# Five slots for the experts' weights instead of three, two of them in memory that the routing stage has used, one packed table of weights, and an earlier turning of the plan

## The chip, the cores and the metric

One core of one Trainium2 chip runs the whole program. The metric is the device time of one execution in microseconds (us). The kernel before took 3438.68 us (median of 3 runs, 3435.18 to 3443.06). One further execution was recorded by the profiler: it took 3445.58 us, its span (first to last instruction) is 3442.7 us. All durations below are from that execution.

## The reference, cut to what matters

Two transformer blocks stand behind each other; the second has two layers. The change touches the mixture of experts at the end of each of these two layers. It works on 512 tokens of 1024 numbers, all float32:

```python
def moe_ffn(h, router_w, router_bias, w_gate, w_up, w_down, ws_gate, ws_up, ws_down):
    scores = sigmoid(xt @ router_w)                       # 512 tokens x 64 experts
    ...                                                   # groups, then the best 8 experts of each token
    wts = wts / sum(wts) * ROUTED_SCALE
    ...
    def run_block(args):                                  # a block of tokens of one expert e
        hb = silu(xb @ w_gate[e]) * (xb @ w_up[e])        # 1024 -> 256, twice
        return (hb @ w_down[e]) * ws[:, None]             # 256 -> 1024
    ...
    shared = (silu(xt @ ws_gate) * (xt @ ws_up)) @ ws_down
    return routed + shared
```

Which experts get how many tokens is known only on the chip. An expert's weights are 3 matrices of 1024 x 256 floats, 1 MB each, 3 MB in all; there are 64 experts.

## The kernel before, in words

Each layer's mixture of experts runs in three stages: `route_tokens`, `routed_experts`, `combine`.

**`route_tokens`** normalises the tokens, scores them, picks the experts and works out a *plan*: rows of `plan` say which expert each pass serves. DVE makes the plan by some 60 small operations on columns (L2589 and near it), ends with `wide` (L2664) and counts `cols_ready`. PE turns `wide` into rows (L2477), DVE copies them into `plan` (L2671) and counts `plan_ready`. SP reads three experts' numbers from it and issues the first loads (`first_loads`, L1899 to L1905). DVE goes on to match seats with tokens (`passes.select`, L1947), PE finds the tokens of the first passes (`passes.find`, L1955 and L1958), and POOL gathers their rows. Beside this PE computes the shared expert in four products of 8 matmuls (`shared_product(j, m)`, L2443): (0,0), (1,0), then the turning of the plan, (0,1) with the first find ahead of its k = 5, the second find, (1,1). The stage's own big buffers are `hT_e`, `shared_up` and `rows_hat`, 16 KB per partition each. The next stage starts when every engine has ended this one.

**`routed_experts`** goes through rounds r = 0, 1, ... Each round has two passes of 128 seats: pass b = 0 serves one expert ("whole"), pass b = 1 serves two of 64 seats each ("first", "second"). There are 47 passes in the first of the two layers and 45 in the second; the last round has pass b = 0 alone. A pass on PE is: turn the gathered rows (L2828), `up` (gate and up matrices, L2842), turn the hidden rows (L2853), `down` (L2866). PE's order, written out by hand: up(r,0), down(r-1,1), turn, up(r,1), down(r,0), turn. Between them stand the finds of later passes. ACT and DVE empty the accumulators, and POOL gathers rows for later passes and scatters the results (L1977, L2784).

The weights lie in `experts`, `[P, 3, EXPERT]`: one slot of 24 KB per partition for each of the three parts, 16 KB of it for gate and up, 8 KB for down. SP loads them in a fixed order: `load_up(r,0)`, `load_down(r-1,1)`, `load_up(r,1)`, `load_down(r,0)`. Each call waits until PE has done the pass of the round before on that slot (L2730: `up_made`, `down_made`), then issues 1 MB DMAs, two for an `up`, one for a `down` (L1910, L1914). A 1 MB DMA writes 8 KB to each of 128 partitions, from one contiguous megabyte of HBM.

**`combine`** sums the 8 results of each token with the shared expert's product and normalises.

Of the kernel before, what the change touches and what calls it, by code (L numbers as in the profile page):

```python
# [20 lines left out]
P = 128  # L21
T = 512
TT = T // P
D = 1024
# [1853 lines left out]
class Experts:  # L1878
# [5 lines left out]
    def __init__(self, prog, ctx, l):  # L1884
        d = prog.dram
        self.l = l
        self.mem = prog.sb(ctx, "experts", [P, 3, EXPERT])
        self.holder, sems = prog.semaphores([f"{part}_loaded_{i}" for part in ("up", "down") for i in range(3)])
        self.up_loaded, self.down_loaded = sems[0:3], sems[3:6]
        self.shared = [d["ws_gate_2"][l], d["ws_up_2"][l], d["ws_down_2"][l]]  # L1890
        self.routed = [d["w_gate_2"], d["w_up_2"], d["w_down_2"]]

    def up(self, slot):
        return self.mem[:, slot, 0:4 * DK * P].rearrange("p (h k n) -> p h k n", h=2, k=DK)

    def down(self, slot):
        return self.mem[:, slot, 4 * DK * P:6 * DK * P].rearrange("p (k n) -> p k n", k=2)

    def first_loads(self, sp, plan):  # L1899


        es = [sp.value_load(plan[0:1, at:at + 1], min_val=0, max_val=EXPERTS - 1) for at in (0, P, P + 1)]
        for slot in range(3):
            self.load_up(sp, slot, es[slot])
        self.load_down(sp, self.WHOLE, es[0])  # L1905
# [7 lines left out]
    def load_down(self, sp, slot, e):  # L1913
        sp.dma_start(self.mem[:, slot, 4 * DK * P:6 * DK * P],  # L1914
                     self.routed[2][self.l, e].rearrange("(p k) n -> p (k n)", p=P)).then_inc(self.down_loaded[slot], 16)

    def retire(self, prog):
        prog.retire(self.holder, self.up_loaded + self.down_loaded)
# [393 lines left out]
def route_tokens(prog, experts, passes, late_norms, mod, xT, rw, rb, shared_down, shared_down_loaded,  # L2312
# [7 lines left out]
    nc, d = prog.nc, prog.dram  # L2320
    gain, shift = late_norms[:, 0, :], late_norms[:, 1, :]
    with ExitStack() as ctx:
        hT = prog.sb(ctx, "hT_e", [P, DK, T])
        shared_up = prog.sb(ctx, "shared_up", [P, 2, DK, FF])
        rows_hat = prog.sb(ctx, "rows_hat", [P, TT, D])
        h_tok = rows_hat
        by_turns = h_tok[:, :, :].rearrange("p t (k a) -> p t a k", k=DK)
        stats = prog.sb(ctx, "stats", [P, TT, 2, 6])
# [33 lines left out]
        with prog.stage("shared_loaded", "folded", "rows_turned", "stats_ready", "moments_ready", "root_ready", "rstd_ready",  # L2362
# [34 lines left out]
            def _(pe):  # L2397
# [38 lines left out]
                def shared_product(j, m, hook=False):  # L2436
                    for k in range(DK):
                        if hook and k == 5:
                            pe.wait_ge(s["plan_ready"], 1)
                            e = experts_of(pe, 0)[0]  # L2440
                            pe.wait_ge(s["matched"], 1)
                            passes.find(pe, 0, e, info, find_ps[0]).then_inc(s["found"], 1)
# [40 lines left out]

            @block.scalar
# [207 lines left out]
def routed_experts(prog, experts, passes, seat, info, plan, base):  # L2692
# [4 lines left out]
    with ExitStack() as ctx:  # L2697
# [12 lines left out]
        y_ps = prog.ps(ctx, "y_ps", [P, 2, T])  # L2710
        with prog.stage("matched", "found", "noted", "read_noted", "turned", "copied_dve", "copied_act",
                        "up_made_0", "up_made_1", "up_made_2", "silu_ready", "hid_ready", "hid_turned", "hid_copied",
                        "down_made_0", "down_made_1", "down_made_2", "write_noted", "y_dve", "y_act", "go", "shared_out", drains=False) as (block, s):
# [3 lines left out]
            whole, first, second = experts.WHOLE, experts.FIRST, experts.SECOND  # L2717

            def end_of(eng):

# [2 lines left out]
            def past(j, n):  # L2723

                return not isinstance(j, int) or j >= n
# [6 lines left out]
            def experts_of(eng, r, b):  # L2732

                return [eng.value_load(plan[0:1, bass.ds(at, 1)], min_val=0, max_val=EXPERTS - 1)
                        for at in ((r,) if b == 0 else (P + 2 * r, P + 2 * r + 1))]

            @block.sync
            def _(sp):
                def load_up(r, b):
                    es = experts_of(sp, r, b)  # L2740
                    if past(r, 1):
                        all_waited(sp, up_made[b], r)
                    for i, e in enumerate(es):
                        experts.load_up(sp, b + i, e)

                def load_down(r, b):
                    es = experts_of(sp, r, b)
                    if past(r, 1):
                        all_waited(sp, down_made[b], 2 * r)
                    for i, e in enumerate(es):  # L2750
                        experts.load_down(sp, b + i, e)

                end = end_of(sp)
                load_up(1, 0)
                load_down(0, 1)
                load_up(1, 1)
                load_down(1, 0)
# [6 lines left out]
                load_up(last, 0)  # L2764
                load_down(end, 1)
                load_down(last, 0)

            @block.gpsimd
            def _(pool):
# [42 lines left out]
            def _(pe):  # L2812
# [19 lines left out]
                def up(r, b):  # L2832
                    j = 2 * r + b
                    for i in range(b + 1):
                        pe.wait_ge(experts.up_loaded[b + i], 32 * (r + 1))
                    pe.wait_ge(s["copied_dve"], j + 1)
                    pe.wait_ge(s["copied_act"], j + 1)
                    if past(j, 2):
                        pe.wait_ge(s["hid_ready"], j - 1)
                    for k in range(DK):  # L2840
                        for i, part in enumerate((ALL,) if b == 0 else halves):
                            made = pe.matmul(up_ps[part, b, :].rearrange("p (h n) -> p h n", h=2), xT[:, b, k, part],  # L2842
                                             experts.up(b + i)[:, :, k, :], start=(k == 0), stop=(k == DK - 1))
                            if k == DK - 1:
                                made.then_inc(up_made[b][i], 1)

# [9 lines left out]
                def down(r, b):  # L2856
                    j = 2 * r + b
                    for i in range(b + 1):
                        pe.wait_ge(experts.down_loaded[b + i], 16 * (r + 1))
                    pe.wait_ge(s["hid_copied"], j + 1)  # L2860
                    for side in range(2):
                        if past(j, 1):
                            pe.wait_ge(s["y_dve"] if side == 0 else s["y_act"], j)
                        for k in range(2):
                            for i, part in enumerate((ALL,) if b == 0 else halves):
                                made = pe.matmul(y_ps[part, side, :], hidT[:, b, k * P + part.start:k * P + part.stop],  # L2866
                                                 experts.down(b + i)[:, k, side * 512:(side + 1) * 512],
                                                 start=(k == 0), stop=(k == 1))
                                if k == 1:
                                    made.then_inc(down_made[b][i], 1)  # L2870
# [492 lines left out]
```

## Time and profile before

| | |
|---|---|
| median of 3 runs | 3438.68 us (3435.18 to 3443.06) |
| the profiled execution | 3445.58 us, span 3442.7 us |
| PE (matmul) busy | 3097.1 us, 90% of the span |
| DVE, ACT, POOL busy | 46%, 29%, 7% |
| DMA | 739.11 MB, mean 215 GB/s over the span |
| expert loads | 137 each of gate, up and down, 1024 KB each |

The page cuts the span into 40 slices of 86 us. Slices 19 to 26 and 32 to 39 are the two `routed_experts` stages: there the DMA engines' busy share is 9 tenths in nearly each, at 350 to 410 GB/s, and PE's is 9 too. Outside them the DMA share is mostly 0 to 6 tenths. "DMA share" is the mean over the core's 16 DMA engines; above 1 it means that transfers overlapped. PEclk is the clock granted to PE as a part of its full speed; it is either full (1.0) or half.

### The profile page before, as it was taken

Reading aid. Unit: us, or ns where it says so; the run is one execution under the profiler, and the core shown is the slowest. Engines: PE = TensorE matmul, PEld = TensorE weight load, DVE = VectorE, ACT = ScalarE, POOL = GpSimd, SP = SyncE. Lnnn points to the kernel's source line nnn. Section 1 sums busy time; section 2 is a strip of 40 time slices with the busy share of each in tenths; the row PEclk is TensorE's granted clock in tenths of the full one; section 3 lists DMA queues with packets and bytes.
Section 4 is the critical chain, followed back from the end, with each engine's and each line's share of the span. In section 5 each row is a group of like instructions: output and inputs, shape, how many; then the busy total and the mean of one; then the engine's idle time right before and its main releaser. Section 6 shows DMA issues by size and latency. Waiting matters only on the chain. (4 is left out here: it accounts for less than half of the span.)

```text
span 3442.7 us, 44956 instructions
## 1 busy us (share of the span) xinstructions
PE 3097.1 (90%) x14116; PEld 1988.1 (58%) x14117; DVE 1596.6 (46%) x4079; ACT 983.0 (29%) x2055; POOL 252.1 (7%) x237
## 2 busy tenths in 40 slices
PE   7888989989999889989999899969899799999995
PEld 4555668878777667864444444366587444444444
DVE  2575466657566365444223323264734532323236
ACT  4565352333233244331111111133632211111111
POOL 0000000011000000000111111100000011111112
PEclk9899999999999999988999999989999899999997
DMA  5201126644543412316999999771031399999985
GB/s 207 75 2 50 48 70 189 209 159 151 184 148 129 131 28 56 104 37 249 402 406 409 399 394 406 305 292 44 26 94 57 149 394 412 396 391 403 386 353 241
DMA packets 283481, 739.11 MB, mean 215 GB/s; under 512 B 25197, under 2 KB 164655, under 8 KB 228555
## 3 DMA queue, kind: packets, MB, share of 16 engines
q1 hardware_dynamic: 231211, 619.79, 47.4%
q0 software_dynamic: 26784, 67.15, 4.9%
q10 hardware_dynamic: 25344, 50.33, 4.3%
q8 instruction: 82, 1.34, 0.2%
q14 instruction: 60, 0.49, 0.0%
HBM read 709.92 MB, written 57.67 MB: 223 GB/s over the span
## 5 line engine op out<-in xcount | busy, mean ns | idle before, releaser
L2842 PE MATMUL up_ps<-experts,x_turned 128*64 128x512 f32 (+1 forms) x2192 | 684.2, 624 | 99.4 <-DMA experts<-in_w_up_dram 80.2
L318 DVE TENSOR_TENSOR pieces_lo<-weights,pieces_hi 128x512 fp32r<-128x512 f32 (+1 forms) x468 | 319.0, 686 | 461.9 <-ACT pieces_hi L312 461.2
L2842 PEld LDWEIGHTS up_ps<-experts,x_turned 128*64 128x64 f32 (+1 forms) x2192 | 264.8, 161 | 449.0 <-issue 444.4
L312 ACT CAST pieces_hi<-weights 128x512 fp32r<-128x512 f32 (+1 forms) x468 | 284.4, 615 | 584.8 <-PE gate_ps L330 174.0
L2866 PE MATMUL y_ps<-experts,hid_turned 128*64 128x512 f32 (+1 forms) x1096 | 338.3, 601 | 2.0 <-issue 2.0
L2997 DVE TENSOR_TENSOR hid_seats<-up_ps,gated 128x256 f32<-128x256 f32 x92 | 56.2, 611 | 566.0 <-ACT gated L2919 566.0
L328 PE MATMUL gate_ps<-h_hi,pieces_hi 128*128 128x512 f32 x624 | 248.7, 399 | 19.3 <-DVE pieces_lo L318 19.3
L2919 ACT ACTIVATE gated<-up_ps 128x256 f32<-128x256 f32 x92 | 35.3, 384 | 761.4 <-PE up_ps L2842 761.4
L329 PE MATMUL gate_ps<-h_lo,pieces_hi 128*128 128x512 f32 x624 | 245.9, 394 | 0.0
L330 PE MATMUL gate_ps<-h_hi,pieces_lo 128*128 128x512 f32 x624 | 245.7, 394 | 0.0
L2866 PEld LDWEIGHTS y_ps<-experts,hid_turned 128*64 128x64 f32 (+1 forms) x1096 | 115.2, 155 | 217.6 <-issue 217.6
L328 PE MATMUL products<-h_hi,pieces_hi 128*128 128x512 f32 x464 | 196.7, 424 | 30.6 <-DVE pieces_lo L318 30.6
L330 PE MATMUL products<-h_hi,pieces_lo 128*128 128x512 f32 x464 | 187.2, 404 | 0.0
L329 PE MATMUL products<-h_lo,pieces_hi 128*128 128x512 f32 x464 | 186.6, 402 | 0.0
L2784 POOL DMA_INDIRECT results<-y_seats,write_at x92 | 92.8, 1009 | 873.6 <-ACT y_seats L2934 873.6
L1947 DVE TENSOR_SCALAR seats<-lists,base,seat 128x64 fp32r<-128x64 f32 (+1 forms) x588 | 146.5, 325 | 20.6 <-issue 20.3
L2934 ACT ACTIVATE y_seats<-y_ps,share 128x512 f32<-128x512 f32 x92 | 63.4, 689 | 310.4 <-PE y_ps L2866 310.4
L328 PEld LDWEIGHTS gate_ps<-h_hi,pieces_hi 128*128 128x128 f32 x624 | 119.1, 191 | 45.0 <-DVE pieces_lo L318 20.5
L845 ACT ACTIVATE prob<-prob,low 128x512 f32<-128x512 f32 (+5 forms) x224 | 123.9, 553 | 66.8 <-DVE low L876 65.9
L2988 DVE COPY x_turned<-turn_ps 128x512 f32<-128x512 f32 x92 | 63.6, 692 | 164.2 <-PE turn_ps L2828 164.2
L328 PEld LDWEIGHTS products<-h_hi,pieces_hi 128*128 128x128 f32 x464 | 90.1, 194 | 82.8 <-issue 40.0
L330 PEld LDWEIGHTS gate_ps<-h_hi,pieces_lo 128*128 128x128 f32 x624 | 119.0, 191 | 25.6
(454 smaller groups left out, 4930.8 us busy)
## 6 DMA issues: line engine op xcount, KB each, us to landing
experts<-in_w_gate_dram SPq DMA_DIRECT2D x137, 1024.0 KB, 8.9
experts<-in_w_up_dram SPq DMA_DIRECT2D x137, 1024.0 KB, 15.6
experts<-in_w_down_dram SPq DMA_DIRECT2D x137, 1024.0 KB, 16.6
ada_weights<-in_w_ada_dram ACTq DMA_DIRECT2D x48, 1024.0 KB, 5.3
rows_sb<-results SPq DMA_DIRECT2D x16, 2048.0 KB, 26.3
weights<-in_w_in_dram SPq DMA_DIRECT2D x57, 512.0 KB, 4.2
weights<-in_w_in_dram SPq DMA_DIRECT2D x12, 2048.0 KB, 12.2
weights<-in_w_out_dram SPq DMA_DIRECT2D x6, 2048.0 KB, 8.8
```

The source lines that it names most:

```text
L312: act.copy(self.like(view, self.hi[:, i % self.BUFFERS, :, :]), view).then_inc(s["hi_ready"], 1)
L318: dve.tensor_tensor(lo, view, hi.bitcast(F32), ALU.subtract).then_inc(s["lo_ready"], 1)
L328: pe.matmul(bank, self.hi[:, b, k, :], x_hi[:, k0 + k, :], start=(start and k == 0), stop=False)
L329: pe.matmul(bank, self.hi[:, b, k, :], x_lo[:, k0 + k, :], start=False, stop=False)
L330: last = pe.matmul(bank, self.lo[:, b, k, :], x_hi[:, k0 + k, :], start=False, stop=(stop and k == n - 1))
L845: act.activation(prob[:, u % 6, 0:x["n"]], prob[:, u % 6, 0:x["n"]], ACT.Exp, bias=low[:, u % 8:u % 8 + 1], scale=-1.0, accum_out=mass[:, ...
L1947: last = dve.tensor_scalar(self.seats[:, b, t, part], prog.count[:, 0:part.stop - part.start], firsts[i], seat[:, t, bass.ds(e, 1)], ALU.a ...
L2784: pool.indirect_dma_start(d["results"], bass.IndirectOffsetOnAxis(ap=write_at[:, b:b + 1], axis=0), y[:, b, :], None, bounds_check=last_ro ...
L2842: made = pe.matmul(up_ps[part, b, :].rearrange("p (h n) -> p h n", h=2), xT[:, b, k, part], experts.up(b + i)[:, :, k, :], start=(k == 0), ...
L2866: made = pe.matmul(y_ps[part, side, :], hidT[:, b, k * P + part.start:k * P + part.stop], experts.down(b + i)[:, k, side * 512:(side + 1) ...
L2934: act.activation(y[:, b, 512:1024], y_ps[:, 1, :], ACT.Copy, scale=share[:, bass.ds(j, 1)]).then_inc(s["y_act"], 1)
L2988: dve.tensor_copy(xT[:, b, 0:4, :].rearrange("p k n -> p (k n)"), turn_ps[:, 0, :]).then_inc(s["copied_dve"], 1)
```

## The change

The host packs, for each layer and expert, the three matrices behind each other by partition (`experts_by_partition`, 24 KB per partition), so that gate and up are one 2 MB DMA with 16 KB per partition. `experts` has five slots. "Whole" and "first" have two each, chosen by the round's parity (`place`), "second" has one. Slots 3 and 4 are also the memory of `hT_e`, `shared_up` and `rows_hat` (`spare`). SP's order of loads is new, with waits on PE of an older round for the doubled parts, a wait for the landing of the part's load before, and a count `asked` ahead of each load. PE reads a doubled part at an address that depends on the round's register. In `route_tokens` PE turns the plan after k = 1 of product (1,0), finds the first pass's tokens after k = 1 of product (0,1) and the second's after its k = 4.

```diff
+def experts_by_partition(given):
+    parts = [given[name].reshape(LAYERS, EXPERTS, P, -1) for name in ("w_gate_2", "w_up_2", "w_down_2")]
+    return np.concatenate(parts, axis=3)
...
-        self.mem = prog.sb(ctx, "experts", [P, 3, EXPERT])
+        self.mem = prog.sb(ctx, "experts", [P, 5, EXPERT])
...
+    def place(self, part, r):
+        return 2 if part == self.SECOND else 3 * (r & 1) + part
+    def spare(self):
+        return self.mem[:, 3:5, :].rearrange("p i n -> p (i n)")
+    def up(self, part, r):
+        slot = self.place(part, r)
+        return self.mem[:, bass.ds(slot, 1), 0:4 * DK * P].rearrange("p s (h k n) -> p (s h) k n", h=2, k=DK)
...
-    def load_up(self, sp, slot, e):
-        for m in range(2):
-            at = 2 * m * DK * P
-            sp.dma_start(self.mem[:, slot, at:at + 2 * DK * P],
-                         self.routed[m][self.l, e].rearrange("(p k) n -> p (k n)", p=P)).then_inc(self.up_loaded[slot], 16)
+    def load_up(self, sp, part, r, e):
+        sp.dma_start(self.mem[:, bass.ds(self.place(part, r), 1), 0:4 * DK * P].rearrange("p s n -> p (s n)"),
+                     self.routed[e, :, 0:4 * DK * P]).then_inc(self.up_loaded[part], 16)
...
-        hT = prog.sb(ctx, "hT_e", [P, DK, T])
-        shared_up = prog.sb(ctx, "shared_up", [P, 2, DK, FF])
-        rows_hat = prog.sb(ctx, "rows_hat", [P, TT, D])
+        spare = experts.spare()
+        hT = spare[:, 0:DK * T].rearrange("p (k n) -> p k n", k=DK)
...
+                        if (j, m, k) == (1, 0, 2):
+                            turn_plan()
+                        if (j, m, k) == (0, 1, 2):
+                            find_first()
+                        if (j, m, k) == (0, 1, 5):
+                            find_second()
...
                 shared_product(0, 0)
                 shared_product(1, 0)
-                pe.wait_ge(s["cols_ready"], 1)
-                pe.wait_ge(s["h_copied"], 2 * TT)
-                for i in range(4):
-                    last = pe.matmul(plan_ps[:, i, :], wide[:, i, :], prog.ident[:, :], start=True, stop=True)
-                last.then_inc(s["plan_turned"], 1)
-                shared_product(0, 1, hook=True)
-                pe.wait_ge(s["matched"], 2)
-                passes.find(pe, 1, None, info, find_ps[1]).then_inc(s["found"], 1)
+                shared_product(0, 1)
                 shared_product(1, 1)
...
-                with sp.Fori(2, last) as r:
-                    load_up(r, 0)
-                    load_down(r - 1, 1)
-                    load_up(r, 1)
-                    load_down(r, 0)
...
+                def load_up(part, r, freed, e):
+                    if past(freed, 1):
+                        sp.wait_ge(up_of[part], freed)
+                        sp.sem_inc(s["asked"], 1)
+                    if part != second:
+                        sp.wait_ge(experts.up_loaded[part], 16 * r)
+                    sp.sem_inc(s["asked"], 1)
+                    experts.load_up(sp, part, r, e)
...
+                def both(r):
+                    n = r + 1
+                    pair = two(n)
+                    load_up(second, n, n, pair[1])
+                    load_down(whole, n, r, one(n))
+                    load_up(whole, n + 1, n, one(n + 1))
+                    load_up(first, n + 1, n, two(n + 1)[0])
+                    load_down(first, n, r, pair[0])
+                    load_down(second, n, n, pair[1])
+
+                load_up(whole, 1, 0, one(1))
+                pair = two(0)
+                load_down(first, 0, 0, pair[0])
+                load_down(second, 0, 0, pair[1])
+                load_up(first, 1, 0, two(1)[0])
+                both(0)
+                with sp.Fori(1, end - 1) as r:
+                    both(r)
...
-                        pe.wait_ge(experts.up_loaded[b + i], 32 * (r + 1))
+                        pe.wait_ge(experts.up_loaded[b + i], 16 * (r + 1))
...
-                                             experts.up(b + i)[:, :, k, :], start=(k == 0), stop=(k == DK - 1))
+                                             experts.up(b + i, r)[:, :, k, :], start=(k == 0), stop=(k == DK - 1))
```

## Rows read from the trace of the kernel before

**Rows 1.** Stretches of both layers: us, busy time (instructions), PEclk, DMA share, GB/s.
```profile
1577.00:1596.00 19.00, 14.42 (x40) 6.94 (x38) 7.83 (x29) 0.60 (x1) 2.21 (x2) 0.88 1.01 405
1596.00:1607.00 11.00, 10.17 (x25) 4.75 (x24) 3.26 (x16) 0.97 (x2) 0.00 (x0) 0.74 0.10 39
1607.00:2223.00 616.00, 568.05 (x2272) 260.83 (x2271) 188.05 (x686) 87.85 (x182) 92.05 (x91) 0.98 0.98 398
2223.00:2236.00 13.00, 11.08 (x35) 3.89 (x33) 2.41 (x7) 2.02 (x4) 0.99 (x1) 1.00 0.06 21
2747.00:2758.00 11.00, 9.84 (x28) 4.94 (x28) 3.84 (x16) 0.67 (x2) 0.00 (x0) 0.84 0.13 54
2758.00:3350.00 592.00, 542.83 (x2168) 246.85 (x2167) 179.43 (x655) 83.99 (x174) 87.83 (x87) 0.97 0.98 398
```

**Rows 2.** Waits, 1595 to 3360: who waited for whom, us in total, times, longest.
```profile
PE up_ps L2842 <- DMA experts<-in_w_up_dram: 80.2, 37, 3.3
...
SPq L2730 <- PE up_ps L2842: 370.7, 43, 12.2
```

**Rows 3.** Timeline of PE: start, us, instruction group, idle before it and releaser.
```profile
1608.72 7.09 PE L2842 MATMUL up_ps<-experts,x_turned 128*64 128x512 f32 x32 [0.32 <-DVE x_turned L2988]
1621.18 7.10 PE L2842 MATMUL up_ps<-experts,x_turned 128*128 128x512 f32 x16 [0.31 <-DVE x_turned L2988]
...
2219.32 7.13 PE L2842 MATMUL up_ps<-experts,x_turned 128*128 128x512 f32 x16 [0.64 <-DVE x_turned L2988]
...
2231.39 3.67 PE L2866 MATMUL y_ps<-experts,hid_turned 128*128 128x512 f32 x8 [0.98 <-issue]
...
3358.49 3.67 PE L2866 MATMUL y_ps<-experts,hid_turned 128*128 128x512 f32 x8 [0.98 <-issue]
```

**Rows 4.** DMA packets and bytes in 1577 to 2223 and in 2728 to 3350.
```profile
DMA packets 43612, 253.34 MB, mean 392 GB/s; under 512 B 8666, under 2 KB 8666, under 8 KB 16725
...
DMA packets 41728, 243.57 MB, mean 392 GB/s; under 512 B 8010, under 2 KB 8010, under 8 KB 15994
```

**Rows 5.** Stretches of 27 us with the DMA share near 1.
```profile
1821.00:1848.00 27.00, 26.17 (x110) 11.88 (x108) 9.34 (x34) 3.87 (x8) 4.05 (x4) 1.00 1.02 422
...
1928.00:1955.00 27.00, 24.62 (x104) 11.44 (x102) 8.36 (x31) 3.87 (x8) 4.05 (x4) 1.00 0.99 401
...
2250.00:2277.00 27.00, 19.36 (x141) 18.45 (x140) 23.64 (x33) 4.18 (x11) 0.00 (x0) 0.87 1.00 427
```

**Rows 6.** Timeline around the plan in the first of the two layers.
```profile
1564.74 0.43 DVE L2664 COPY wide<-chosen_unit 128x512 f32<-128x512 f32 x1
...
1565.57 0.60 ACT L2508 ACTIVATE silu<-banks 128x512 f32<-128x512 f32 x1 [13.47 <-PE banks L2443]
1572.24 1.05 PE L2477 MATMUL banks<-square,wide 128*128 128x128 f32 x8
...
1575.98 0.38 SPq L1910 DMA_DIRECT2D experts<-in_w_gate_dram  x1
...
1580.04 0.65 PE L1955 MATMUL banks<-info,seats 128*128 x4 [2.45 <-DVEq L2681]
...
1585.27 7.11 PE L2443 MATMUL banks<-hT_e,shared_up 128*128 128x512 f32 x16
```

**Rows 7.** The same in the second layer.
```profile
2717.96 0.43 DVE L2664 COPY wide<-chosen_unit 128x512 f32<-128x512 f32 x1
...
2723.69 1.05 PE L2477 MATMUL banks<-square,wide 128*128 128x128 f32 x8
```

**Rows 8.** Register work of PE's sequencer for the first find: ns min/median/max.
```profile
L1955 PEldq FUSED_REGOPS  x188: 46/46/51, 1579.9 to 3319.0; - x188
```

**Rows 9.** Gathers of POOL: times, us from issue to landing.
```profile
x_seats<-tokens,read_at POOLq DMA_INDIRECT x94, 9.1
```

**Rows 10.** Timeline: POOL gathers for pass b = 0; PE turns these rows.
```profile
2005.10 1.02 POOL L1977 DMA_INDIRECT x_seats<-tokens,read_at  x1 [2.85 <-DVE read_at L1966]
...
2026.01 1.04 PE L2828 MATMUL turn_ps<-square,x_seats 128*128 128x128 f32 x8
```

More of the change, by code:

```diff
@@ L1890, in __init__ @@
         self.shared = [d["ws_gate_2"][l], d["ws_up_2"][l], d["ws_down_2"][l]]
[L1891 to L1897, printed above, removed]
+        self.routed = d["experts_by_partition"][l]
+    def place(self, part, r):
+        return 2 if part == self.SECOND else 3 * (r & 1) + part
@@ L1899, in first_loads, with down @@
+    def spare(self):
[3 more added lines that the diff above has]
+        return self.mem[:, bass.ds(slot, 1), 0:4 * DK * P].rearrange("p s (h k n) -> p (s h) k n", h=2, k=DK)
+    def down(self, part, r):
+        slot = self.place(part, r)
+        return self.mem[:, bass.ds(slot, 1), 4 * DK * P:6 * DK * P].rearrange("p s (k n) -> p (s k) n", k=2)
     def first_loads(self, sp, plan):
         es = [sp.value_load(plan[0:1, at:at + 1], min_val=0, max_val=EXPERTS - 1) for at in (0, P, P + 1)]
-        for slot in range(3):
-            self.load_up(sp, slot, es[slot])
@@ L1905, in first_loads @@
-        self.load_down(sp, self.WHOLE, es[0])
-    def load_up(self, sp, slot, e):
-        for m in range(2):
-            at = 2 * m * DK * P
-            sp.dma_start(self.mem[:, slot, at:at + 2 * DK * P],
-                         self.routed[m][self.l, e].rearrange("(p k) n -> p (k n)", p=P)).then_inc(self.up_loaded[slot], 16)
-    def load_down(self, sp, slot, e):
-        sp.dma_start(self.mem[:, slot, 4 * DK * P:6 * DK * P],
-                     self.routed[2][self.l, e].rearrange("(p k) n -> p (k n)", p=P)).then_inc(self.down_loaded[slot], 16)
+        for part in range(3):
+            self.load_up(sp, part, 0, es[part])
@@ L2434, in turn_h, with turn_plan, find_first, find_second @@
                     last.then_inc(s["h_turned"], 1)
-                def shared_product(j, m, hook=False):
-                    for k in range(DK):
[L2438 to L2442, printed above, removed]
+                def turn_plan():
+                    pe.wait_ge(s["cols_ready"], 1)
+                    pe.wait_ge(s["h_copied"], 2 * TT)
+                    for i in range(4):
+                        last = pe.matmul(plan_ps[:, i, :], wide[:, i, :], prog.ident[:, :], start=True, stop=True)
+                    last.then_inc(s["plan_turned"], 1)
+                def find_first():
+                    pe.wait_ge(s["plan_ready"], 1)
+                    e = experts_of(pe, 0)[0]
+                    pe.wait_ge(s["matched"], 1)
+                    passes.find(pe, 0, e, info, find_ps[0]).then_inc(s["found"], 1)
+                def find_second():
+                    pe.wait_ge(s["matched"], 2)
+                    passes.find(pe, 1, None, info, find_ps[1]).then_inc(s["found"], 1)
+                def shared_product(j, m):
+                    for k in range(DK):
+                        if (j, m, k) == (1, 0, 2):
[4 more added lines that the diff above has]
+                            find_second()
                         last = pe.matmul(shared_ps[j][m], shared_up[:, j, k, m * P:(m + 1) * P], hT[:, k, :],
@@ L2712, in routed_experts @@
                         "up_made_0", "up_made_1", "up_made_2", "silu_ready", "hid_ready", "hid_turned", "hid_copied",
[L2713 removed]
+                        "down_made_0", "down_made_1", "down_made_2", "write_noted", "y_dve", "y_act", "go", "asked", "shared_out", drains=False) as (block, s):
             scattered = passes.scattered
@@ L2753, in _, with load_down @@
+                def load_down(part, r, freed, e):
+                    if past(freed, 1):
+                        sp.wait_ge(down_of[part], 2 * freed)
+                        sp.sem_inc(s["asked"], 1)
+                    if part != second and past(r, 1):
+                        sp.wait_ge(experts.down_loaded[part], 16 * r)
+                    sp.sem_inc(s["asked"], 1)
+                    experts.load_down(sp, part, r, e)
                 end = end_of(sp)
-                load_up(1, 0)
-                load_down(0, 1)
@@ L2756, in _, with one, two @@
-                load_up(1, 1)
-                load_down(1, 0)
                 last = end + 1
-                with sp.Fori(2, last) as r:
-                    load_up(r, 0)
-                    load_down(r - 1, 1)
-                    load_up(r, 1)
-                    load_down(r, 0)
-                load_up(last, 0)
-                load_down(end, 1)
-                load_down(last, 0)
+                def one(r):
+                    return experts_of(sp, r, 0)[0]
+                def two(r):
+                    return experts_of(sp, r, 1)
@@ new lines, in _ @@
+                load_down(first, 0, 0, pair[0])
[4 more added lines that the diff above has]
+                    both(r)
+                pair = two(end)
+                load_up(second, end, end, pair[1])
+                load_down(whole, end, end, one(end))
+                load_up(whole, last, end, one(last))
+                load_down(first, end, end, pair[0])
+                load_down(second, end, end, pair[1])
@@ L2768, in _ @@
+                load_down(whole, last, end, one(last))
             @block.gpsimd
@@ L2866, in down @@
                                 made = pe.matmul(y_ps[part, side, :], hidT[:, b, k * P + part.start:k * P + part.stop],
-                                                 experts.down(b + i)[:, k, side * 512:(side + 1) * 512],
+                                                 experts.down(b + i, r)[:, k, side * 512:(side + 1) * 512],
                                                  start=(k == 0), stop=(k == 1))
@@ L3356 @@
     given["x_turned"] = features_by_partition(given["x"][0])
+    given["experts_by_partition"] = experts_by_partition(given)
+    for name in ("w_gate_2", "w_up_2", "w_down_2"):
+        del given[name]
     for name, a in given.items():
```

19 lines of the change are left out of this document (7 added, 12 removed).

## The prediction, written before the result was known

> **What bounds the kernel now.** I read the page's slices first, then the stretches of the two expert stages [rows 1], the waits [rows 2] and PE's timeline [rows 3]. The page alone says "PE 90%", which would make a change of loads worthless. The stretches say more: from 1607 to 2223 and from 2758 to 3350 the DMA share is 0.98 at 398 GB/s while PE is busy 92% of the time; both are nearly full. The waits tell which is the tighter: PE waits for an expert's up weights 37 times, 80.2 us in total [rows 2]. Where it doesn't wait, one pass follows the other after 12.46 us (1608.72 to 1621.18), so a round takes 24.9 us [rows 3]. From 1608.72 to the last up at 2219.32 there are 45 passes in 610.60 us, 13.57 each, so 27.1 us a round. SP in turn waits 370.7 us for PE to free a slot [rows 2]: with one slot per part the load of a round can't start before PE has ended the same part of the round before. Thus DMA and PE hold each other up, and the DMA stands nearly idle for 11 us at each stage's start (shares 0.10 and 0.13), because the next load needs the first pass of the stage to end [rows 1].
>
> **The change, part by part.** Sums are against the profiled execution (3445.58 us, span 3442.7), which lies 6.9 us above the median of 3438.68; I take the same difference off the median.
>
> *a. More slots.* In the new order PE's end of up(n-1,1) releases loads of second up, whole down, whole up, first up, first down: 8 MB of the round's 9, and the ninth 1 MB load waits for down(n-1,1), some 17 us on, well before 8 MB are through (8 x 1.049 MB at 412 GB/s is 20 us). When PE waits for data, SP's next release is already past, so the queue doesn't run dry. I therefore price the stage as the bytes over the rate of a full queue. The bytes stay: 253.34 and 243.57 MB, gathers and scatters included [rows 4]. The rate in full stretches of 27 us lies between 401 and 422 GB/s [rows 5]; I take the middle, 412, as either end is a single stretch. 253.34/0.412 = 615 us, 243.57/0.412 = 591 us. Gaps that stay: from the end of the first loads to the new stage's first load, and once before PE's first release of "second"; I estimate 5 us together in place of the 11 and more. So 620 in place of 646 us, and 596 in place of 622: 26 us less in each layer.
>
> *b. Two 1 MB loads become one of 2 MB with 16 KB per partition.* In a full queue the bytes count, not the number of loads. The one stretch that moves 16 KB rows, `combine`'s reading of results, runs at 427 GB/s [rows 5]; that is one end. The other end is below 401: the new source steps 24 KB from row to row instead of being contiguous, which no row shows. I take 0, nearest to the rows of these loads themselves. The Trainium skill, "DMA: Bandwidth & Descriptors", section "Bandwidth", gives some 2.0 us fixed per DMA and 341 GB/s for single 1 MB transfers. By it, 137 DMAs fewer would save 274 us. By the rows, 392 GB/s with 1 MB loads over whole stages [rows 4], the fixed part is hidden behind other transfers, and the saving is 0. The trace disagrees with the rule as a sum.
>
> *c. The end of a stage.* Now PE ends 12.1 us after the last load landed (2235.06 against 2223; 3362.16 against 3350) [rows 1, 3], because PE was behind in its own order. With DMA as the bound only the last two downs (3.67 each, the first of them can start 2.5 us before the last landing) stand behind it: 6 us. That is 6 less in each layer.
>
> *d. The plan's turning.* `wide` is complete at 1565.17; product (0,0) is read from 1565.57, so it ended just before; two matmuls of the next product at 7.11/8 = 0.89 us bring PE to 1567.1 instead of 1572.24 [rows 6]: 5.1 us. In the second layer `wide` ends at 2718.39, so 2718.6 instead of 2723.69 [rows 7]: 5.1 us, here the DVE chain sets it. SP's first load follows with it (1575.98 to about 1570.9). PE's wait of 2.45 us before the first find is covered by six matmuls more (5.3 us), and the stage ends some 3 us earlier. The DMA bound counts the 5.1. The gathers are issued about 5 us earlier too, so they don't hold the stage's start.
>
> *e. Register addresses on PE.* Every matmul of a doubled part gets an address worked out from r. The find has such an operand, one register operation of 46 ns per matmul [rows 8]; an up or down matmul takes 0.44 to 0.89 us, so behind the first of a group they are hidden, at 0.1 us for each of the 4 groups of a round, 18 us in both layers. If each took several operations they could reach 0.4 us a group, 72 us. While DMA is the bound, both hide behind it (PE has 24.9 us of work in a round of about 26.5). I take 0 and keep 18 for PE's bound.
>
> *f. `asked`, waits for landing, reads of the plan on SP.* Per load they are a few operations on a queue that waits hundreds of us. The wait for the same part's load of the round before looks back at least 9 MB of loads. 0; below, a rival.
>
> *g. Gathers beside longer rows.* A gather's 4 KB rows share the DMA engines with 16 KB instead of 8 KB rows. The trace has 9.1 us to landing [rows 9]; a doubling to 18 us is the upper end. Its rows are turned 20.9 us after the issue (2005.10 to 2026.01) [rows 10], so 0.
>
> Sum: 26 + 6 + 5 = 37 us in each layer, 74 in both: 3445.6 - 74 = 3372 profiled, **3365 us** by the median.
>
> **Rivals.**
>
> *A. PE becomes the bound.* If the full queue gives 427 GB/s as in `combine`'s stretch, DMA needs 593 and 570 us, 42 us less again, and PE can't follow. PE's own floor: 45 passes at 12.46 us are 561 instead of 610.6, so 50 less, and 3 at the start, 53; for the second layer the same. 106 less, plus 18 of register work: 88 less, **3351 us**. For it: the single stretches at 422. Against: the mean of both stages, 398 at a share of 0.98.
>
> *B. The new source layout is slower (other side).* Place: each 16 KB and 8 KB row read from HBM at a pitch of 24 KB. The gain of 74 is used up when 497 MB take 74 us more than 1206, at 388 GB/s, 6% under 412. At 380 GB/s it is 102 more: 28 slower, **3467 us**. For it: nothing shows this pattern. Against: rows of 8 KB and more are long already. The Trainium skill, same page, section "Latency and other measured facts", reports such a loss for row pitches of 2 MiB and more at powers of two. By that rule a 24 KB pitch costs nothing. No run here shows it.
>
> *C. The full queue has only the 401 GB/s end.* Then 632 and 607 us, 33 more: 41 less, **3398 us**. For it: 401 stands in a stretch with a share of 0.99. Against: the share above 1 where it is 422.
>
> *D. SP blocks its own queue:* one of its waits for a landing holds all loads behind it, and only the earlier start is left, some 10 us: **3429 us**. Against: part f.
>
> **Chances.** Forecast 0.56, A 0.19, C 0.13, D 0.04, B 0.08. What this kernel's measurement can tell from no change is 0.2%, 7 us. D is half faster, half the same. So faster 0.90, same 0.02, slower 0.08. Range: from PE's floor without register work and a little beyond (106 less is 3333, I take 3336) to C, 3400; outside are B, D and the tails.
>
> **What would show it.** Right: the DMA share is 1.0 from the stage's start, with no 11 us hole at 1596; each stage's bytes at about 412 GB/s; PE's waits for loads are less than 80 us and stand before `down` of pass b = 1 rather than before its up; `wide` to the plan's turning under 2.5 us; half-clock stretches rarer. For A: waits of PE for DMA near 0 and 12.5 to 12.9 us a pass. For B: share 1 and under 390 GB/s. For D: a low share while SP waits for a landing. Wrong altogether would be a PE that waits neither for data nor for DVE and still needs more than 13.2 us a pass: then the register addresses cost what e puts at its upper end.

## The result: 1% faster, two fifths of what was forecast

The changed kernel takes **3405.93 us** (median of 4, 3400.05 to 3411.81) against 3437.66 for the kernel before (4 runs, 3435.18 to 3443.06): ratio **0.991** [0.990, 0.992], 32 us less. Forecast were 74 less, 3365, in a range of 3336 to 3400. The direction was right, the size wrong, and the time lies outside the range. The profiled execution took 3406.53 us, its span 3404.4.

Stretches of the kernel after, in the columns of [rows 1]: from the first weight load until first passes begin, the 11 us that follow, the rest until the last load has landed, and what is left; first layer, then second.

```profile
1568.00:1590.00 22.00, 18.45 (x54) 8.78 (x53) 9.86 (x37) 1.18 (x2) 2.21 (x2) 0.94 0.98 400
1590.00:1601.00 11.00, 10.65 (x35) 5.46 (x35) 2.63 (x10) 1.24 (x3) 0.97 (x1) 0.80 1.01 427
1601.00:2201.00 600.00, 554.96 (x2260) 249.11 (x2261) 186.46 (x683) 86.92 (x180) 91.08 (x91) 1.00 0.97 400
2201.00:2213.00 12.00, 10.66 (x34) 3.69 (x32) 2.40 (x7) 1.38 (x4) 0.99 (x1) 1.00 0.06 22
2702.00:2722.00 20.00, 16.45 (x51) 7.96 (x49) 7.78 (x28) 1.18 (x2) 2.08 (x2) 0.97 0.97 404
2722.00:2733.00 11.00, 11.00 (x28) 5.31 (x28) 2.79 (x13) 0.38 (x1) 0.00 (x0) 0.75 1.01 425
2733.00:3311.00 578.00, 530.22 (x2161) 238.01 (x2160) 177.89 (x649) 83.92 (x174) 87.84 (x87) 1.00 0.97 398
3311.00:3327.00 16.00, 13.40 (x40) 4.98 (x38) 3.84 (x13) 2.02 (x4) 0.99 (x1) 1.00 0.12 43
```

The hole where [rows 1] have it is filled: shares 1.01 and 1.01 for 0.10 and 0.13. A shorter one has taken its place, some 14 us later when counted from the first load, inside the long stretches. These lines show it, then what lies behind it, then (last line) the same middle in the kernel before:

```profile
1603.00:1609.00 6.00, 6.00 (x27) 2.25 (x24) 0.42 (x1) 0.38 (x1) 0.90 (x1) 1.00 0.35 118
1620.00:2190.00 570.00, 526.16 (x2160) 235.78 (x2160) 176.49 (x643) 83.06 (x172) 87.05 (x86) 1.00 0.99 407
...
1620.00:2213.00 593.00, 546.02 (x2185) 250.27 (x2185) 179.53 (x656) 84.14 (x175) 89.06 (x88) 0.98 0.99 402
```

In the second layer the short hole lies at 2737 to 2743 (share 0.45). Behind the holes the rate is 407 GB/s at a share of 0.99 where it was 402 at 0.99: more slots, with the longer rows, have made the middle hardly faster. A stage's loads take 632 and 610 us (646 and 621 before) where the forecast had 620 and 596.

Waits from 1585 to 3330, in the columns of [rows 2]:

```profile
PE y_ps L2917 <- DMA experts<-xperts_by_partition_dram: 38.4, 28, 2.3
PE up_ps L2893 <- DVE x_turned L3039: 32.2, 61, 1.5
PE up_ps L2893 <- DMA experts<-xperts_by_partition_dram: 23.8, 31, 0.8
...
SPq L2778 <- PE y_ps L2917: 344.5, 45, 14.0
```

TensorE still waits 62.2 us for loads (38.4 + 23.8), only 18 less than the 80.2 of [rows 2]. The waits have moved, as forecast, mostly in front of the down product.

Packets, queues and landings of the kernel after from 1568 to 2201 (queue 1: weights; queue 0: gathers and scatters; then count, MB, share of 16 engines; last lines: count and median us to landing):

```profile
DMA packets 33553, 253.28 MB, mean 400 GB/s; under 512 B 7567, under 2 KB 7567, under 8 KB 15628
...
q1 hardware_dynamic: 20155, 220.13, 84.2%
q0 software_dynamic: 13388, 33.04, 13.2%
...
experts<-xperts_by_partition_dram SPq DMA_DIRECT2D x68, 2048.0 KB, 23.1
experts<-xperts_by_partition_dram SPq DMA_DIRECT2D x70, 1024.0 KB, 21.6
x_seats<-tokens,read_at POOLq DMA_INDIRECT x48, 12.7
```

A load lands 22 to 23 us after its issue, so outside the short hole loads are always queued (the trace has no gap of 1 us between packets of weights there). Yet the two queues fill only 97.4% of the 16 engines' time, and the rate stays under the 422 GB/s that [rows 5] have within a stage. That is the question of this case: who idles in a queue that does not run dry?

The plan, TensorE's pass, and the first stage's end, in three timelines:

```profile
1560.89 0.43 DVE L2690 COPY wide<-chosen_unit 128x512 f32<-128x512 f32 x1
...
1563.14 1.05 PE L2455 MATMUL banks<-square,wide 128*128 128x128 f32 x8
...
1566.90 1.48 SPq L1924 DMA_DIRECT2D experts<-xperts_by_partition_dram  x3
```
```profile
1651.43 7.09 PE L2893 MATMUL up_ps<-experts,x_turned 128*64 x32 [0.37 <-DVE x_turned L3039]
1658.44 3.70 PE L2917 MATMUL y_ps<-experts,hid_turned 128*128 x8
1664.09 7.13 PE L2893 MATMUL up_ps<-experts,x_turned 128*128 x16 [0.52 <-DVE x_turned L3039]
```
```profile
2196.89 7.13 PE L2893 MATMUL up_ps<-experts,x_turned 128*128 x16 [0.89 <-DVE x_turned L3039]
2203.95 3.65 PE L2917 MATMUL y_ps<-experts,hid_turned 128*64 x16
2207.53 0.44 PE L2904 MATMUL hid_ps<-square,hid_seats 128*128 128x128 f32 x2
2209.05 3.69 PE L2917 MATMUL y_ps<-experts,hid_turned 128*128 x8 [1.08 <-issue]
```

`wide` to its turning takes 2.25 us (7.50 in [rows 6]). An unhindered pass takes 12.66 us (1651.43 to 1664.09), 0.2 more than the 12.46 of [rows 3]. At the end TensorE is still 12 us behind the last landing at 2200.3.

### The profile page after: what moved, and what is told of

Its sections match the earlier page's. It is cut to its first block and busy times, and to the rows that moved or that the text cites. A ratio compares the mean times of both kernels' runs of the same rounds, so it can differ in the third digit from the quotient of the medians.

```text
span 3404.4 us, 46521 instructions
## 1 busy us (share of the span) xinstructions
PE 3067.9 (90%) x14116; PEld 1967.1 (58%) x14117; DVE 1595.6 (47%) x4079; ACT 982.9 (29%) x2055; POOL 252.1 (7%) x237
## 5 line engine op out<-in xcount | busy, mean ns | idle before, releaser
L2893 PE MATMUL up_ps<-experts,x_turned 128*64 128x512 f32 (+3 forms) x2192 | 659.4, 599 | 56.0 <-DVE x_turned L3039 32.2
L2893 PEld LDWEIGHTS up_ps<-experts,x_turned 128*64 128x64 f32 (+1 forms) x2192 | 245.4, 156 | 400.1 <-issue 400.1
L2917 PE MATMUL y_ps<-experts,hid_turned 128*64 (+3 forms) x1096 | 340.0, 604 | 42.4 <-DMA experts<-xperts_by_partition_dram 38.4
```

## Experiments

Gathers and scatters move only the rows of filled seats (an empty seat's address lies out of bounds), and seats are filled from partition 0 up. Thus partitions 0, 1, 2, ... of a pass carry rows in every pass, the last ones in few. If each DMA engine serves its own partitions, some carry more than others, and as a weight load goes over all 128 partitions, it lands when the most loaded engine is done with it. Prediction step a divided bytes by the rate of all 16 together, which can't show this.

I take an engine to have partitions p to p+3 and p+32 to p+35; the permutations below bear that out. With that map and the routing of the inputs (a count over experts' tokens, no row of the profile) the heaviest engine has 351 of the first layer's 4096 rows, the lightest 131, the mean is 256. Queue 0's 13.2% of 16 x 633 us over 8192 rows (4096 in, 4096 out) is 0.163 us a row: 114, 43 and 83 us. Weights add 84.2% of 633, 533 us. The heaviest comes to 647 us, the mean to 616; at the share of 1.01 that full stretches show, 640 and 610. Spread seats come near the mean but don't reach it: by the same count the heaviest engine has 277 rows in seats_by_port and 270 in seats_spread, 617 and 615 us at 1.01. Measured are 632 with seats in order and 609 with either spread (table). Each is 6 to 8 us under its sum, and the 23 us from seats in order to seats_by_port are the distance of their sums.

The Trainium skill, "DMA: Bandwidth & Descriptors", section "The descriptor swizzle", states this same map for a load over 128 partitions; that it holds for gathers and scatters too is what seats_by_port and seats_reversed show.

All results in one table; us are (ratio - 1) times the 3440 us of the kernel before, loads' us are from the first weight load to the last landing, first and second layer.

| kernel | median us (runs) | ratio to before [95%] | us | loads' us |
|---|---|---|---|---|
| before | 3437.7 to 3441.2 | 1 | 0 | 646, 621 |
| after | 3405.93 (4) | 0.9909 [0.9896, 0.9922] | -31 | 632, 610 |
| seats_spread | 3360.10 (5) | 0.9760 [0.9742, 0.9779] | -83 | 609, 582 |
| seats_by_port | 3356.39 (5) | 0.9753 [0.9735, 0.9771] | -85 | 609, 583 |
| seats_reversed | 3382.42 (5) | 0.9828 [0.9812, 0.9844] | -59 | 621, 594 |
| gathers_full | 3406.62 (6) | 0.9897 [0.9881, 0.9914] | -35 | 634, 610 |
| before_spread | 3392.76 (5) | 0.9862 [0.9843, 0.9882] | -47 | 620, 594 |
| plan_early | 3432.46 (12) | 0.9971 [0.9960, 0.9982] | -10 | 645, 621 |
| plan_late | 3416.49 (6) | 0.9925 [0.9908, 0.9942] | -26 | 631, 609 |
| packed_three | 3428.44 (7) | 0.9959 [0.9945, 0.9974] | -14 | 639, 616 |
| unpacked_five | 3415.47 (6) | 0.9924 [0.9908, 0.9940] | -26 | 637, 613 |
| two_loads | 3416.57 (6) | 0.9923 [0.9906, 0.9939] | -26 | 636, 613 |
| three_slots_spread | 3372.47 (5) | 0.9798 [0.9781, 0.9815] | -69 | 616, 590 |
| turn_ahead | 3360.16 (5) | 0.9758 [0.9741, 0.9774] | -83 | 609, 583 |

### Seats dealt to other partitions: seats_spread, seats_by_port, seats_reversed, before_spread

The seat number that a partition of a pass holds becomes a permutation. What is computed stays the same:

```
-    count = np.broadcast_to(np.arange((T // P + 1) * P, dtype=np.float32), (P, (T // P + 1) * P))
+    count = np.arange((T // P + 1) * P, dtype=np.float32)
+    count[0:P] = SEAT_OF_WHOLE
+    count[P:P + P // 2] = SEAT_OF_HALF
+    count = np.broadcast_to(count, (P, (T // P + 1) * P))
...
-  dve.tensor_scalar(self.seats[:, b, t, part], prog.count[:, 0:part.stop - part.start], firsts[i],
+  dve.tensor_scalar(self.seats[:, b, t, part], prog.count[:, b * P:b * P + part.stop - part.start], firsts[i],
```

In seats_spread the permutation evens out the rows under three maps of partitions to engines at once, in seats_by_port under the one map above alone; seats_reversed has the bits of the partition's number reversed; before_spread is seats_spread's edit on the kernel before.

> The changed kernel, with only the order of seats over partitions altered: the first, nearly always filled seats of a pass are spread over all partitions instead of lying in the low ones. Bytes and instructions are the same. Counted from this input's routing, with seats in order the partitions served by one DMA engine take up to 351 gathered rows a layer and those of another 131, mean 256. Theory 1 (the most loaded DMA engine sets the stage, since every load needs all 16): the heaviest engine loses some 25 us of gather and scatter work a layer, so the time falls by 30 to 50 us, to about 3365, the landings of one load come closer together, the rate rises from 395 to over 405 GB/s. Theory 2 (the mean rate of the full queue is simply lower than I took): no change within 5 us.

> As seats_spread, but balanced only if an engine serves four partitions and the four 32 further on (88 us of gather and scatter on the heaviest by that count, against 112 before), and not if it serves 8 neighbouring ones (116 us). Theory 1 with the first way of serving: as fast as seats_spread, some 3365. Theory 1 with 8 neighbours: no gain, 3406. Theory 2: 3406.

> The kernel before with the seats spread as in seats_spread. Theory 1: it gains as well, some 20 to 50 us (3390 to 3418), since its loads also need all 16 engines. Theory 2: 3438, no change.

Measured: 3360.10 and 3356.39, 46 and 50 us less than the changed kernel; on the kernel before 47 less. Stretches of seats_by_port, cut as above without the ends, and its waits:

```profile
1587.00:1598.00 11.00, 11.00 (x29) 5.37 (x29) 2.77 (x13) 0.38 (x1) 0.00 (x0) 0.75 1.00 426
1598.00:2175.00 577.00, 553.44 (x2263) 248.84 (x2263) 187.25 (x684) 87.77 (x182) 92.06 (x91) 1.00 1.00 416
2700.00:2711.00 11.00, 11.00 (x32) 5.32 (x30) 2.62 (x12) 0.61 (x2) 0.21 (x1) 0.76 1.01 427
2711.00:3262.00 551.00, 528.62 (x2161) 237.54 (x2160) 178.92 (x654) 83.67 (x174) 87.63 (x87) 1.00 1.00 418
```
```profile
PE up_ps L2900 <- DVE x_turned L3046: 41.3, 89, 1.5
...
PE y_ps L2924 <- DMA experts<-xperts_by_partition_dram: 4.0, 6, 1.0
```

The same bytes go at 416 and 418 GB/s in place of 400 and 398, the share is 1.00 with the short hole still in these stretches, and TensorE's waits for loads fall from 62.2 us to 4.0. Nothing was taken out of the queue; the rows only go through other engines.

The first expectation named a second sign, that the landings of one load come closer together, and the kept traces bear it out. A weight load signals its landing in 16 parts. From the first to the last of a load's 16 signals the median is 12.1 and 12.7 us in the changed kernel (first and second layer), 10.8 and 11.1 in seats_reversed, 7.5 and 4.4 in seats_by_port; in the kernel before it is 5.2 and 5.2, in before_spread 3.0 and 3.4. So some engines do run behind the others, and less so with spread seats.

> The changed kernel with seats dealt to partitions in bit-reversed order, a dose between the order 0,1,2,... and the spread ones. If a load's 128 partitions are served by 16 engines, each with four partitions and the four that lie 32 further on, then the most loaded engine has 312 and 305 filled rows in the two layers, against 351 and 348 in the changed kernel and 256 in the spread ones: 100 and 98 us of gathers and scatters at 0.16 us a row each way, against 112 and 111, and 82. Theory of the most loaded engine: 12 to 14 us per layer less, 3382 us (3374 to 3388). Rival, that each engine serves eight neighbouring partitions: 93 and 90 us, nearly all of the gain, 3362. Rival, that partitions are dealt out by their number modulo 16: 119 us against 92, slower than the changed kernel by 40 us or more.

Measured 3382.42, on the forecast of 3382. In order of the heaviest engine's rows (351, 312, and 277 in seats_by_port; the expectation's 256 is the mean) the first layer's loads take 632, 621 and 609 us: 11 less for the 12.7 us of rows taken off the heaviest engine, then 12 less for 11.4. Both rival maps are out: by the one 3362 was due, by the other a slower kernel.

### More rows on the lightly loaded engines: gathers_full

Every empty seat gathers token 511 (rows that nothing reads back out); the scatters stay:

```
-  out[part, 4 * i:4 * i + 1], float(T), None, ALU.add)
+  out[part, 4 * i:4 * i + 1], float(T), float(T - 1), ALU.add, ALU.min)
```

> The changed kernel with the token index of an empty seat clamped to the last token, so that the gathers move all 128 rows instead of the filled ones: some 1900 rows of 4 KB more a layer, 8 MB. What is computed for filled seats is the same. Theory 1: the heaviest engine's seats are filled already, so at most 3 us a layer, 3406 to 3412. Theory 2 (mean bytes over a rate): 8 MB at 400 GB/s are 20 us a layer, 3446.

Queues of gathers_full from 1567 to 2202:

```profile
q1 hardware_dynamic: 20160, 220.21, 83.0%
q0 software_dynamic: 13387, 41.42, 16.3%
```

8.4 MB more went through in the first layer (41.42 for 33.04) and the loads took 634 for 632 us, 412 GB/s on average: 3406.62 us, as the changed kernel. So it was not the number of bytes that set the pace, nor a rate that all bytes share. Extra rows on engines with idle time were free here; the heaviest engine had 351 of its 376 seats (8 in each of 47 passes) filled and got 25 rows more, 4 us.

### One part of the change at a time: plan_early, plan_late, packed_three, unpacked_five, two_loads

plan_early and packed_three put one part into the kernel before; plan_late and unpacked_five take one out of the kernel after. The code moved is that of the change itself. two_loads is the changed kernel with this:

```
-  sp.dma_start(mem[..., 0:4 * DK * P], self.routed[e, :, 0:4 * DK * P]).then_inc(self.up_loaded[part], 16)
+  for at in (0, 2 * DK * P):
+      sp.dma_start(mem[..., at:at + 2 * DK * P], self.routed[e, :, at:at + 2 * DK * P]).then_inc(self.up_loaded[part], 16)
```

> The kernel before with one part of the change: the routing plan turned inside the shared product (loads, slots and weight layout as before). The prediction's step d says 5.1 us per layer. In the changed kernel the wide-to-turned stretch fell from 7.50 to 2.25 us and the first weight load came 4.6 us earlier against its layer's clock in layer 1 and 3.5 us in layer 2. If the load stage is only shifted and not changed, the time falls by 7 to 10 us against the kernel before (ratio 0.9972 to 0.9980). If the rival holds, that the earlier start is eaten by the stage's end (its loads are limited by something that does not start earlier), it is within 3 us of before.

> The changed kernel with the plan turned where it was before, all else changed. Step d undone: 7 to 10 us slower than the changed kernel, 3413 to 3416 us. If the plan's place only matters with three slots (rival), it equals the changed kernel, 3406.

The early plan is worth 10 us added (within some 4) and 5 taken away (within some 7, so not clear of noise); the loads' stretches keep their length (645 and 621; 631 and 609) and are only shifted.

> The kernel before with one other part: three slots, but the weights read from the table laid out by partition, gate and up of an expert as one 2 MB load. Step b took nothing for it. With the most loaded DMA engine as the limit, what counts is the bytes per engine, which are the same: then 3437 us, within 4 us of before. But the full queue moved 425 GB/s in the changed kernel with spread seats and 420 in the kernel before with spread seats, and one load instead of two removes one completion per pass: if that is the layout's doing, 1.2% of two 600-us stretches less idle share, 5 to 10 us faster. If fewer, larger loads hurt with three slots (a slot is free later, since gate and up wait for each other), slower by 5 us or more.

> The changed kernel with five slots and the early plan, but the weights in their three matrices and two 1 MB loads for gate and up. Step b undone. If layout and load size are worth nothing: 3406 us within 4. If they carry the 425 against 420 GB/s: 5 to 12 us slower. Together with packed_three and plan_early the rest of the 31.7 us is the worth of the slots: I expect 15 to 23 us for these, against the 52 that step a forecast, since the most loaded engine bounds the stage.

> The changed kernel with its table by partition, but gate and up of an expert as two loads of 1 MB. With three separate matrices and two loads the changed kernel took 9 us longer, and the kernel before took 12.8 us less with table and single load. If it is the number of loads and of packets: 3412 to 3416, as with the separate matrices. If it is the place of the bytes in memory (one expert's rows of one partition beside each other): 3406, as the changed kernel.

Table and single load are worth 14 us added and 5 taken away (within some 7 again); the loads' stretches, one profile each, agree better: 12 us shorter over both layers (639 and 616 for 646 and 621), some 7 longer when undone. two_loads has the new table and the old number of loads, and can't be told from unpacked_five (0.9923 and 0.9924; 636 and 613 us for 637 and 613). So the gain comes from the one longer load with 16 KB rows. The 24 KB pitch of the new table neither costs nor gives anything measurable. Whether the longer row or the missing second load does it, no run tells apart, but the packets point to the row: in the first layer of the changed kernel a 16 KB packet takes 0.632 us on the mean, in two_loads an 8 KB one 0.320. Over the packets of the first layer's loads that is 5 us less work for each engine, and the stretch is 4 us shorter.

### What the slots are worth once engines are even: three_slots_spread

This is the kernel before with the early plan, the table with one load, and the seats of seats_by_port.

> What the change keeps without its slots: three slots (the loads and their waits of the kernel before), with the early plan, the weight table by partition with one 2 MB load, and the seats dealt by port as in the best kernel so far (3356.4). The kernel before with spread seats took 3392.8. Less 9 for the plan and 9 to 13 for the layout: 3371 to 3375, and five slots would then be worth 15 to 19 us where engines are evenly loaded. Rival: with even engines a slot is free in time whatever the number of slots, so that this reaches 3356 to 3360, and the slots are worth nothing. Step a forecast 52 us for the slots.

Measured 3372.47, in the forecast 3371 to 3375: the two further slots are worth 16 us (0.9798 to 0.9753, within some 8). Stretches of three_slots_spread, around the stage's start and after it:

```profile
1596.00:1607.00 11.00, 11.00 (x29) 5.38 (x29) 2.81 (x13) 0.38 (x1) 0.00 (x0) 0.75 0.03 6
1607.00:2191.00 584.00, 557.39 (x2266) 254.72 (x2266) 187.44 (x684) 87.86 (x182) 92.06 (x91) 0.99 1.01 420
```

The hole of 11 us is back (share 0.03), and behind it three slots keep the queue as full as five (420 GB/s, share 1.01). Loads take 616 and 590 us against 609 and 583: 7 us per layer. That is about the long hole less the short one that five slots still have: the weights' queue is empty for 10.4 and 11.4 us here and for 4.7 and 4.8 in seats_by_port. Middle of the stage: nothing.

### TensorE's wait for turned tokens taken away: turn_ahead

seats_by_port with the turning moved ahead of the down product, and the copies ahead of the weighing on ScalarE and VectorE:

```
     up(r, 0)
+    turn(r, 1)
     down(r - 1, 1)
-    turn(r, 1)
```

> The fastest kernel so far (changed kernel, seats dealt by port, 3356.4 us) with TensorE turning the next tokens before the down product instead of after it, and ScalarE and VectorE copying them before they weigh the outputs. There the pass takes 12.62 and 12.67 us nearly throughout and TensorE waits 41.3 us in 89 passes for the copy of the turned tokens. If TensorE's own work now sets the pass, each pass falls by 0.4 to 0.5 us to 12.2; the queue then has to carry 253.3 and 243.6 MB at its full 425 GB/s, 596 and 573 us, against stages of 608.6 and 582.8 now: 8 to 22 us less in all, 3334 to 3348, I say 3344. Rival: loads are the bound already, 3356 within 3, with waits for loads in the place of those for the copy.

My forecast of 3344 missed: 3360.16, no less than seats_by_port. Its waits:

```profile
PE up_ps L2900 <- DMA experts<-xperts_by_partition_dram: 35.1, 30, 1.6
...
PE y_ps L2924 <- DMA experts<-xperts_by_partition_dram: 5.3, 6, 1.2
```

The 41.3 us of waits for the copy are gone and 40.4 us of waits for loads stand in their place. The loads' stretches are unchanged at 609 and 583 us. The rival holds: with even engines loads and TensorE are so close that, with TensorE's wait gone, the queue is the limit. The fastest version run is seats_by_port, **3356.39 us**, 2.5% under the kernel before (0.9753 [0.9735, 0.9771]) and some 1.5% under the change (seats_spread and turn_ahead can't be told from it).

## Why the prediction was wrong in size

**Step a failed: the stage was priced as all bytes over the mean rate of a full queue, 412 GB/s.** It gave 26 us per layer: 6 for the hole (11 us shrunk to the 5 us of gaps that stay) and 20 for a faster rest (635 us of loads at 398 GB/s become 615 at 412). The hole came as priced, about 7 us per layer by three_slots_spread, and the gap that stays is there: the weights' queue is empty for 5.6 and 4.8 us at the short hole. The faster rest did not come, because the queue's mean rate is not the limit; the most loaded engine is. It had the same rows and weights to carry with three slots as with five. The rows read for this step may have held the sign: a stretch at 422 and one at 401 with shares of 1.02 and 0.99 [rows 5] need not be two draws around a mean, they can be engines together and engines apart. I took the middle, and with it a gain that slots can't give. Rival C had the measured rate (401, against 400) and with 3398 the nearest time, for no stated cause; it deserved more than 0.13.

**Step c was wrong.** I took 6 us off the end of each stage, arguing that TensorE would no longer be behind its order. It ends 12 us after the last landing in the first layer and 14 in the second, against 12 before. When the last load lands at 2200, TensorE is 3 us into the last up (from 2196.89), and the rest of it, two downs and a turning stand in its order, until 2212.74. That is its own work and hardly any wait, and even engines don't shorten it: in seats_by_port the last load lands at 2175 and the last down ends at 2188.

**Step d was right in the first layer and too high in the second.** From `wide` to the turning it is 5.25 us less in the first (7.50 to 2.25) and 3.37 in the second (5.73 to 2.36), for 5.1 forecast in each; the first load follows `wide` 5.2 and 3.0 us sooner. plan_early bears the sum out with 10 us.

**Step b was taken as 0 and is worth 5 to 14 us.** The argument that only bytes count in a full queue failed by some 0.5 to 1%. The fear behind rival B, a slower source, found no support: two_loads and unpacked_five can't be told apart. The 2.0 us per DMA that the prediction quoted from the Trainium skill stand, on the page that it names, in the section "Anatomy of one DMA — SWDGE (gpsimd) path", not in "Bandwidth"; the saving of 274 us by them did not come either.

**Steps e, f, g had the right size.** With register addresses passes take 12.67 and 12.62 us in turn (seats_by_port), without them 12.52 and 12.45 (three_slots_spread): 0.16 us a pass for the forecast 0.2. It stands as idle time before the up (0.52 us for 0.30 in pass b = 0, 0.32 for 0.22 in b = 1), not in the matmuls; that the addresses cause it is likely but not isolated, as these two kernels also differ in their slots. It is hidden while loads bind. SP did wait for landings in the changed kernel, 75.2 us in 36 waits and 43.9 in 31, none over 2.8 us, but this emptied no queue, and seats_by_port has such waits at full rate too (51.8 us in 28). A gather lands after 12.7 us instead of 9.0, and TensorE shows no wait for it.

The sum by what the loads' stretches and the plan show, both layers: slots 13 to 15 (forecast 52), one load instead of two 7 to 12 (0), plan 8 (10), end 0 (12): 28 to 35 us, around the 31 measured. That rival C came near is luck: the price of the rest was wrong, and no rival named an engine that others wait for.

What remained open: no row names each DMA engine, so that the heaviest one's load is worked out from the routing and borne out by three permutations and the spread of landings, not read off. Whether the limit of such a group of partitions lies in its engine or in its way into the memory is not told apart. Why the longer load helps is shown only by its packets.

## What to carry to other kernels

A queue that doesn't run dry has not thereby reached its rate. Here its middle showed a share of 0.98 to 0.99 and 399 to 407 GB/s with uneven engines, 1.01 to 1.02 and 416 to 424 with even ones. Such a small gap is worth a count: add up bytes engine by engine before more buffers are bought. Where indirect transfers skip rows, deal the used rows out over the partitions; it cost one constant here and gave 46 us, more than the whole change. And price a buffer by the hole that it closes in the stretches, less the hole that stays: two slots against a hole of 11 us were worth 7 us a layer here.

## What the runs showed of the hardware

An indirect gather or scatter uses, for each partition, the same engine as a long load does: its partitions p to p+3 and p+32 to p+35. The dose of seats_reversed and the time of seats_by_port show these groups of partitions; that what they share is the engine is the simplest reading. A 4 KB row costs its engine 0.163 us by the queue's share. Even engines carry 416 to 418 GB/s over a stage of mixed loads and gathers, and 424 between 1750 and 2150 (seats_by_port). With 1 MB loads in 8 KB rows a stage takes 3 to 7 us longer than with 2 MB loads in 16 KB rows.
